# Gated attention: value products one step later, behind the transpositions, and both behind the gate burst

## The chip, the cores and the metric

The kernel runs on one core of a Trainium2 chip. The metric is the time of one execution on the device in microseconds (us). The core has five engines that run side by side and meet only at semaphores: TensorE (PE; its weight loads are shown apart, as PEld), VectorE (DVE), ScalarE (ACT), GpSimd (POOL) and SyncE (SP), which issues most of the transfers here.

## The reference

The program computes two transformer blocks one after the other on 1024 tokens of width 1024. The change lies in the second block, in the mixer that runs three kinds of attention and gates what they give:

```
for h in 4 heads:   fox:    p = softmax(causal(q k^T / 8 + decay));   y = p v
for h in 4 heads:   lstm:   w = (q k^T) * exp(decay);  y = w v / max(|w 1|, floor), then an RMS norm
for h in 8 heads:   window: p = softmax(band(q k^T / 8 + bias), sink); y = p v      # 128 keys back
gates = sigmoid(h @ w_gates)              # [1024 tokens, 4 * 1024]
merged = sum over 4 branches of gate * (y_branch @ w_branch)
```

The products `h @ w_gates` are the large ones of this stage. They need no attention result, so the kernel runs them between the steps of the attention.

## The kernel before

The function `gated_attention` holds the stage. It has one stream of instructions for each engine, written out by hand, and semaphores between them.

**Steps.** There are N = 128 steps, one for a block of 128 queries of one head: steps 0 to 31 are the fox heads, 32 to 63 the decay heads (`lstm`), 64 to 127 the window heads. A step t of a fox head has t + 1 blocks of 128 keys, a window step has two (the first of a head has one). On TensorE a fox or window step has three parts. `score` makes the scores of a step in PSUM. `turn_probs` transposes its probabilities, block by block, into the PSUM tile `turned`. `multiply` makes the value products from the transposed copy `pt` (shown as `ga_row` in the trace). A decay step has `score` and then `add_up`, with no transposition.

**Other engines in a step.** VectorE's `shift` reads the scores and writes the tile `probs` (shown as `ga_p`); the next `score` waits for it (`shifted`), since there is one tile of scores. ScalarE's `exponentials` work in place on `probs`, and ScalarE's `copy_turned` copies `turned` to `pt`. In a decay step VectorE's `weigh` takes the place of `shift`. After each head, VectorE scales the eight results (`scale_head`) or divides them (`divide`); the first product of the next head waits for that.

**Gate bursts.** The gate products are 112 products of 4 chunks; a chunk is three matmuls of 512 columns (high and low parts of both operands, lines 238 to 240). The 448 chunks are cut into 131 bursts, and `gates(s + 1)` is the burst of step s, with 3 or 4 chunks:

```
bounds = [N_GATE * PART * i // BURSTS for i in range(BURSTS + 1)]
ends = [max(i for i in range(BURSTS) if bounds[i] <= q * PART + PART - 1) - 1 for q in range(N_GATE)]
split_at = {step: q + RING for q, step in enumerate(ends) if q + RING < N_GATE}
```

The weights of a product stand in a ring of two (`RING = 2`) as a high and a low part. ScalarE casts the high part of product q + 2 (`high_part`, line 4160) in the step in which product q ends, and VectorE subtracts it for the low part (`low_part`, line 4257). A product's first chunk waits for its low part (`lows`) and for the evacuation of the product two before it.

**Order on ScalarE.** In step s it goes through these, each where the step has it: row copies, `copy_turned(s - 1)`, `exponentials(s)`, `leave` (evacuates every fourth product of the first half), `high_part`, `swap_high` (casts a part of the tokens' blocks). VectorE's order is `shift(s)`, the head's scaling, the norm, gains and convolution where they fall, `leave`, `low_part`, `swap_low`.

**Order on TensorE.** It can be read at the end of the block for `nc.tensor` below: `score(s)`, `turn_probs(s - 1)`, `gates(s + 1)`, `multiply(s - 1)`, and at some steps `turn_rows`, which transposes finished rows.

Of the kernel before, what the change touches and what calls it, by code (L numbers as in the profile page):

```python
# [33 lines left out]
ST = S // P  # L34
# [3673 lines left out]
def gated_attention(k, HT, v2, vm, biases, sinks, fox_y, ml_y, swa_y, first_gates, lower):  # L3708

    nc = k.nc  # L3710
    HEADS, N = 4, SLOTS
# [3 lines left out]
    with k.phase() as ctx:  # L3715
# [36 lines left out]
        rows_a = k.X[:, 0:2, :].rearrange("p a (t n) -> p (a t) n", n=4 * HD)  # L3752
# [14 lines left out]
        def kind_of(n):  # L3767
            return "fox" if n < 4 * ST else "lstm" if n < 8 * ST else "window"
# [22 lines left out]
        def head_target(g):  # L3791
            if g == 0:
                return k.first_fox_head_in, 16 * 8
            loads = sum(8 if h < 4 else 6 if h < 8 or h % 4 == 0 else 2 for h in range(2 - g % 2, g + 1, 2))
            return head_in[g % 2], 16 * loads
# [5 lines left out]
        BURSTS = N + 3  # L3801
# [17 lines left out]
        for n in range(4):  # L3819
            c, tokens = swaps[n]  # L3820
# [44 lines left out]
                return evacuated, m + 1  # L3865
            return added, adds_of(m, q - first_of(m)) if m < PAIRS else adds_of(m, {A22_T4: 1, S3_T3: 3, S4_B22: 4}[i])

        y_groups = [("fox", rows_a, fox_y, c, q, 35 + 2 * c + q, 1 + 2 * c) for c in range(2) for q in range(2)]
        y_groups += [("lstm", rows_b, ml_y, c, q, 71 + 2 * c + q, 4) for c in range(2) for q in range(2)]
        y_groups += [("window", (rows_a, rows_b)[c // 2], swa_y, c, q, 64 + 16 * (c + 1) + 2 + q, 8 + 2 * c + 2)  # L3870
                     for c in range(4) for q in range(2)]
# [183 lines left out]
        @block.tensor  # L4055
        def _(pe):
            def score(n):
                g, t = n // ST, n % ST
                pe.wait_ge(*head_target(g))
                if n:  # L4060
                    pe.wait_ge(shifted, n)
                width, key = (S - t * P, t * P) if kind_of(n) == "lstm" else (chunks_of(n) * P, first(n) * P)
                own, other, other_low, own_again = own_of(g), other_of(g), other_low_of(g), own_again_of(g)
                for at in range(0, width, HALF):
                    to = min(at + HALF, width)
                    nc.tensor.matmul(scores[:, at:to], own[:, t * P:(t + 1) * P], other[:, key + at:key + to],
                                     start=True, stop=False)
                    last = nc.tensor.matmul(scores[:, at:to], own_again[0:HD + 4, t * P:(t + 1) * P],
                                            other_low[0:HD + 4, key + at:key + to], start=False, stop=True)
                last.then_inc(products, 1)  # L4070

            def turn_probs(n):
                pe.wait_ge(exps, n + 1)
                pe.wait_ge(copied, turned_count(n))
                if n == 8 * ST:
                    pe.wait_ge(scaled, 8)
                for c in range(chunks_of(n)):
                    last = nc.tensor.transpose(turned[:, c, :], probs[n % 2][:, c * P:(c + 1) * P], k.ident[:])
                last.then_inc(turns, 1)

            def multiply(n):
                g, t = n // ST, n % ST
                pe.wait_ge(copied, turned_count(n) + 1)
                if t == 0 and g:
                    pe.wait_ge(scaled, g)
                col = g * HD if g < 4 else 4 * HD + (g - 8) // 4 * HD
                for c in range(chunks_of(n)):
                    last = nc.tensor.matmul(head_out[:, t, :], pt[:, c, :], v2[:, first(n) + c, col:col + HD],
                                            start=(c == 0), stop=(c == chunks_of(n) - 1))
                last.then_inc(values, 1)  # L4090

            def add_up(n):
                g, t = n // ST, n % ST
                pe.wait_ge(shifted, n + 1)
                if t == 0:
                    pe.wait_ge(scaled, g)
                    pe.wait_ge(copied, 4 * ST)
                for c in range(t + 1):
                    last = nc.tensor.matmul(lstm_out(t), w[c][:, (t - c) * P:(t - c + 1) * P], vm[:, c, g - 4, :],
                                            start=(c == 0), stop=(c == t))  # L4100
                last.then_inc(values, 1)

            def lstm_out(t):
                return turned[:, t // 4 * 4:t // 4 * 4 + 4, :].rearrange("p c n -> p (c n)")[
                    :, t % 4 * (HD + 1):(t % 4 + 1) * (HD + 1)]

            def turn_rows(i):
                kind, rows, _, c, q, _, ready = y_groups[i]
                pe.wait_ge(normed if kind == "lstm" else scaled, ready)
                if i:  # L4110
                    pe.wait_ge(*y_evacuated(i - 1))
                for t in range(4):
                    last = nc.tensor.transpose(y_turned[:, t, :], rows[:, 4 * q + t, c % 2 * P:(c % 2 + 1) * P], k.ident[:])
                last.then_inc(y_turns, 1)

            def gates(burst):
                for x in range(bounds[burst], bounds[burst + 1]):
                    q, c = x // PART, x % PART
                    m, i = gate_order[q]
                    chunks, tokens = block_of[i]  # L4120
                    if c == 0:
                        pe.wait_ge(lows, q + 1)
                        if q >= 2:
                            pe.wait_ge(*evacuation(q - 2))
                        if m in (0, PAIRS) and i in swap_of:
                            pe.wait_ge(k.block_lows, swap_of[i])
                        if m == PAIRS and i == S4_B22:
                            pe.wait_ge(k.blocks_in[2], 32)
                    last = add_product(nc, gate_ps[q % 2][:], part(weights[q % RING], slice(None), c, slice(None)),
                                       part(part(HT, slice(None), chunks, tokens), slice(None), c, slice(None)), c == 0, c == PART - 1)  # L4130
                    if c == PART - 1:
                        last.then_inc(gate_products, 1)

            gates(0)
            for s in range(END):
                if s < N:
                    score(s)
                if 1 <= s <= N and kind_of(s - 1) != "lstm":
                    turn_probs(s - 1)
                if s + 1 < BURSTS:  # L4140
                    gates(s + 1)
                if 1 <= s <= N:
                    if kind_of(s - 1) == "lstm":
                        add_up(s - 1)
                    else:
                        multiply(s - 1)
                if s in y_at:
                    turn_rows(y_at[s])

# [101 lines left out]
        def _(dve):  # L4251
# [61 lines left out]
            def weigh(n):  # L4313
                g, t = n // ST, n % ST
                dve.wait_ge(products, n + 1)
                dve.wait_ge(exps, n + 1)
                dve.wait_ge(values, g * ST)
                width = S - t * P
                nc.vector.scalar_tensor_tensor(out=w[t], in0=scores[:, 0:width], scalar=HD ** -0.5, in1=probs[n % 2][:, 0:width],
                                               op0=ALU.mult, op1=ALU.mult).then_inc(shifted, 1)  # L4320
# [75 lines left out]
            for s in range(END + 1):  # L4396
                if s < N and kind_of(s) != "lstm":
                    shift(s)
                if s + 1 < N and kind_of(s + 1) == "lstm":
                    mask(s + 1)  # L4400
                if s < N and kind_of(s) == "lstm":
                    weigh(s)
                if s % ST == 1 and s > ST:
                    g = s // ST - 1
                    if 4 <= g < 8:
                        divide(g)
                    else:
                        scale_head(g)
                for h in range(4):
                    if s == (4 + h + 1) * ST + 3:  # L4410
                        mean_square(h)
                    if s == (4 + h + 1) * ST + 5:
                        normalise(h)
                if s - 1 in y_at and y_groups[y_at[s - 1]][0] == "lstm":
                    gain_rows(y_at[s - 1])
                if s in conv_step:
                    convolve(*conv_step[s])
                if s in evac_at:
                    leave(evac_at[s])
                if s in split_at:  # L4420
                    low_part(split_at[s])
                if s in swap_at:
                    for part_index in swap_at[s]:
                        swap_low(part_index)
# [957 lines left out]
```

## Time and profile before

| | us |
|---|---|
| median of the runs (3) | 3155.11 (3154.7 to 3161.17) |
| the profiled execution's own time | 3152.55 |
| its span, first to last instruction | 3150.6 |
| the gated attention stage in it | about 1738 to 2276 |

All of it comes from one profiled execution. Times in the rows are us from the start of the span, durations in us unless marked ns. The share PEclk is the clock that TensorE was granted: 1.00 is 2.4 GHz, and the lower level is 1.2 GHz, so a stretch with both has a value between 0.5 and 1.

### The profile page before, as it was taken

How to read it: one execution, taken by the hardware profiler on the slowest of the kernel's cores; microseconds unless marked ns; L12 is line 12 of the kernel's file. 1: busy time of each engine (PE TensorE's matmuls, PEld its weight loads, DVE VectorE, ACT ScalarE, POOL GpSimd, SP SyncE). 2: the span in 40 equal slices, each digit the busy share in tenths (PEclk: the TensorE clock that was granted, in tenths of full speed). 3: DMA queues.
4: the chain of work that ended last, by engine and by line, in shares of the span. 5: the costliest groups of instructions: out<-in, count | busy, mean ns of one | idle time of the engine just before them, and what ended most of it. 6: DMA issues, size and time to landing. Idle time of an engine off the chain costs nothing. (4 is left out here: it accounts for less than half of the span.)

```text
span 3150.6 us, 40756 instructions
## 1 busy us (share of the span) xinstructions
PE 2950.7 (94%) x14913; PEld 2454.7 (78%) x14913; DVE 1993.9 (63%) x2874; ACT 1568.3 (50%) x2502; POOL 557.5 (18%) x452
## 2 busy tenths in 40 slices
PE   7998999898969999969999999989999899999999
PEld 6766999686858888858777888777787778888887
DVE  5436888523768888874542445565576676666685
ACT  5325788533548888864531444434444332323443
POOL 0001210000233333321422111123200032222000
PEclk9999999899979999989999999999999999999999
DMA  3344221302168888763354545477664233333643
GB/s 110 88 133 121 61 61 32 114 21 103 61 236 297 288 298 289 279 214 111 114 167 130 135 126 163 144 241 224 205 229 141 67 100 109 107 101 114 240 154 114
DMA packets 304553, 475.69 MB, mean 151 GB/s; under 512 B 48675, under 2 KB 196202, under 8 KB 291814
## 3 DMA queue, kind: packets, MB, share of 16 engines
q1 hardware_dynamic: 279718, 427.70, 42.7%
q10 hardware_dynamic: 9088, 28.58, 2.3%
q0 software_dynamic: 15552, 16.82, 1.9%
q8 instruction: 121, 1.98, 0.3%
q14 instruction: 74, 0.61, 0.1%
HBM read 410.55 MB, written 125.87 MB: 170 GB/s over the span
## 5 line engine op out<-in xcount | busy, mean ns | idle before, releaser
L2856 DVE TENSOR_TENSOR moe_wgu_low<-moe_raw,moe_wgu_high 128x2048 fp32r<-128x2048 f32 x94 | 211.2, 2289 | 47.3 <-ACT moe_wgu_high L2793 45.2
L238 PE MATMUL ga_gate<-second_h_high,ga_ws_high 128*128 128x512 f32 x448 | 190.2, 425 | 15.2 <-DVE ga_ws_low L4257 12.2
L2793 ACT ACTIVATE moe_wgu_high<-moe_raw 128x2048 fp32r<-128x2048 f32 x92 | 171.3, 1910 | 20.2 <-ACT moe_y L2802 20.2
L239 PE MATMUL ga_gate<-second_h_low,ga_ws_high 128*128 128x512 f32 x448 | 179.5, 401 | 0.0
L240 PE MATMUL ga_gate<-second_h_high,ga_ws_low 128*128 128x512 f32 x448 | 179.5, 401 | 0.0
L2964 POOL DMA_INDIRECT moe_rows<-scratch_ffn_rows,slot_of_block x47 | 110.5, 2351 | 223.5 <-PE moe_turned L2746 120.0
L238 PE MATMUL up_bank<-second_h_high,up_w_high 128*128 128x512 f32 x352 | 138.7, 394 | 10.5 <-DVE up_w_low L3574 7.3
L238 PE MATMUL pr_acc<-second_h_high,pr_ws_high 128*128 128x512 f32 x336 | 137.8, 410 | 4.9 <-DVE pr_stage L3291 4.1
L240 PE MATMUL up_bank<-second_h_high,up_w_low 128*128 128x512 f32 x352 | 138.4, 393 | 0.0
L239 PE MATMUL up_bank<-second_h_low,up_w_high 128*128 128x512 f32 x352 | 138.2, 393 | 0.0
L240 PE MATMUL pr_acc<-second_h_high,pr_ws_low 128*128 128x512 f32 x336 | 131.9, 393 | 0.0
L239 PE MATMUL pr_acc<-second_h_low,pr_ws_high 128*128 128x512 f32 x336 | 131.8, 392 | 0.0
L3616 DVE TENSOR_TENSOR X<-X,up_bank 128x512 f32<-128x512 f32 x132 | 90.7, 687 | 63.4 <-PE up_bank L240 59.9
L4283 DVE TENSOR_TENSOR ga_stage<-ga_stage,ga_gate 128x512 f32<-128x512 f32 x96 | 65.8, 685 | 95.5 <-PE ga_gate L240 59.1
L238 PE MATMUL down_acc<-second_h_high 128*128 128x512 f32 x300 | 116.7, 389 | 0.0
L239 PE MATMUL down_acc<-second_h_low,second_h_high 128*128 128x512 f32 x300 | 116.7, 389 | 0.0
L240 PE MATMUL down_acc<-second_h_high,second_h_low 128*128 128x512 f32 x300 | 116.7, 389 | 0.0
L2812 ACT ACTIVATE moe_down_ws_high<-moe_raw_down 128x1024 fp32r<-128x1024 f32 x94 | 99.7, 1062 | 31.6 <-PE moe_down L240 31.6
L1687 ACT ACTIVATE twin_pt<-twin_turned 128x512 f32<-128x512 f32 (+1 forms) x192 | 86.8, 487 | 55.8 <-PE twin_turned L1573 54.6
L238 PEld LDWEIGHTS ga_gate<-second_h_high,ga_ws_high 128*128 128x128 f32 x448 | 87.2, 195 | 32.1 <-DVE ga_ws_low L4257 13.5
L2867 DVE TENSOR_TENSOR moe_down_ws_low<-moe_raw_down,moe_down_ws_high 128x1024 fp32r<-128x1024 f32 x94 | 110.6, 1217 | 1.8 <-ACT moe_down_ws_high L2812 1.7
L238 PE MATMUL up_bank<-up_t_high,up_w_high 128*128 128x512 f32 x264 | 103.0, 390 | 1.4 <-DVE up_w_low L3574 1.4
(676 smaller groups left out, 8608.1 us busy)
## 6 DMA issues: line engine op xcount, KB each, us to landing
moe_raw<-in_w_expert_gate_dram SPq DMA_DIRECT2D x32, 1024.0 KB, 5.0
moe_raw<-in_w_expert_up_dram SPq DMA_DIRECT2D x32, 1024.0 KB, 7.1
moe_raw_down<-in_w_expert_down_dram SPq DMA_DIRECT2D x32, 1024.0 KB, 7.4
scratch_gates<-ga_stage SPq DMA_DIRECT2D x96, 256.0 KB, 3.2
scratch_expert_rows<-moe_y ACTq DMA_DIRECT2D x46, 512.0 KB, 5.1
ga_w<-in_w_in_dram SPq DMA_DIRECT2D x92, 256.0 KB, 3.7
scratch_hidden<-X SPq DMA_DIRECT2D x77, 256.0 KB, 2.2
down_rows<-scratch_hidden SPq DMA_DIRECT2D x73, 256.0 KB, 2.9
```

What stands on the lines that cost most here:

```text
L238: nc.tensor.matmul(out, w[0], x[0], start=start, stop=False)
L239: nc.tensor.matmul(out, w[0], x[1], start=False, stop=False)
L240: return nc.tensor.matmul(out, w[1], x[0], start=False, stop=stop)
L1687: nc.scalar.activation(turned_sb[p % 4][:, 0:end - start, :], turned[p % 2][:, 0:end - start, :], ACT.Copy).then_inc(copied, 1)
L2793: nc.scalar.activation(wgu[i % 2][0][:, :, m, :], raw[(2 * i + m) % RAW][:].rearrange("p (c n) -> p c n", n=FF), ACT.Copy).then_inc(up_hig ...
L2812: nc.scalar.activation(w_down[0][:, c * D:(c + 1) * D], raw_down[i % RAW_DOWN][:, c * D:(c + 1) * D], ACT.Copy).then_inc(down_highs, 1)
L2856: nc.vector.tensor_tensor(wgu[i % 2][1][:, :, m, :], raw[(2 * i + m) % RAW][:].rearrange("p (c n) -> p c n", n=FF), wgu[i % 2][0][:, :, m, ...
L2867: nc.vector.tensor_tensor(w_down[1][:, c * D:(c + 1) * D], raw_down[i % RAW_DOWN][:, c * D:(c + 1) * D], w_down[0][:, c * D:(c + 1) * D], ...
L2964: k.nc.gpsimd.indirect_dma_start(out=rows[i % 2][:], out_offset=None, in_=k.scratch["ffn_rows"], in_offset=bass.IndirectOffsetOnAxis(ap=sl ...
L3616: nc.vector.tensor_tensor(out, x, bank_at(f, bank_i), ALU.add).then_inc(combos, 1)
L4283: nc.vector.tensor_tensor(stage[t][:], prior[:], bank[:], ALU.add).then_inc(added, 1)
```

## The change

In the loop over the steps TensorE's order becomes `score(s)`, `gates(s + 1)`, `turn_probs(s - 1)`, `multiply(s - 2)`, and then `add_up(s - 1)` for a decay step. The scaling of fox and window heads moves one step later, and the row transpositions of the fox heads wait for one more scaling in the count. Waits that would close a circle in the first decay head are dropped: `weigh` and `add_up` wait for values and scaling only from the second decay head on.

```
@@ y_groups
-        y_groups = [("fox", rows_a, fox_y, c, q, 35 + 2 * c + q, 1 + 2 * c) for c in range(2) for q in range(2)]
+        y_groups = [("fox", rows_a, fox_y, c, q, 35 + 2 * c + q, 2 + 2 * c) for c in range(2) for q in range(2)]
@@ add_up
                 if t == 0:
-                    pe.wait_ge(scaled, g)
+                    if g > 4:
+                        pe.wait_ge(scaled, g)
                     pe.wait_ge(copied, 4 * ST)
@@ block.tensor, the loop over s
                 if s < N:
                     score(s)
+                if s + 1 < BURSTS:
+                    gates(s + 1)
                 if 1 <= s <= N and kind_of(s - 1) != "lstm":
                     turn_probs(s - 1)
-                if s + 1 < BURSTS:
-                    gates(s + 1)
-                if 1 <= s <= N:
-                    if kind_of(s - 1) == "lstm":
-                        add_up(s - 1)
-                    else:
-                        multiply(s - 1)
+                if 2 <= s <= N + 1 and kind_of(s - 2) != "lstm":
+                    multiply(s - 2)
+                if 1 <= s <= N and kind_of(s - 1) == "lstm":
+                    add_up(s - 1)
                 if s in y_at:
                     turn_rows(y_at[s])
@@ weigh
-                dve.wait_ge(values, g * ST)
+                if g > 4:
+                    dve.wait_ge(values, g * ST)
@@ block.vector, the loop over s
-                if s % ST == 1 and s > ST:
-                    g = s // ST - 1
-                    if 4 <= g < 8:
-                        divide(g)
-                    else:
-                        scale_head(g)
+                if s % ST == 1 and 4 * ST < s - ST < 8 * ST:
+                    divide(s // ST - 1)
+                if s % ST == 2 and s > ST and not 4 * ST < s - ST < 8 * ST:
+                    scale_head(s // ST - 1)
```

## Rows read from the trace of the kernel before

**Rows 1.** Windows: stretch, length, busy time (instructions) by engine, PEclk, DMA share, GB/s.

```profile
1738.00:1886.00 148.00, 145.34 (x871) 127.11 (x870) 65.95 (x125) 72.28 (x141) 18.25 (x15) 1.00 0.49 131
2021.00:2276.00 255.00, 232.09 (x1234) 196.31 (x1233) 149.31 (x306) 105.29 (x274) 69.01 (x51) 0.95 0.71 215
```

**Rows 2.** Waits of TensorE's weight loads, 1735 to 2275: total, times, longest.

```profile
PEld ga_gate L238 <- DVE ga_ws_low L4257: 7.1, 2, 5.8
...
PEld ga_out L4088 <- ACT ga_row L4182: 4.0, 3, 2.5
...
PEld ga_turned L4078 <- ACT ga_p L4188: 1.2, 4, 0.4
```

**Rows 3.** Timeline, a fox step: start, us, engine, line, operation, tiles, count.

```profile
1803.68 0.19 PEld L4066 LDWEIGHTS ga_scores<-x_rounded 128*128 128x128 f32 x1
...
1804.49 0.92 PEld L4078 LDWEIGHTS ga_turned<-ident,ga_p 128*128 128x128 f32 x7
...
1805.69 0.92 ACT L4182 ACTIVATE ga_row<-ga_turned 128x896 f32<-128x896 f32 x1 [2.27 <-PE ga_turned L4078]
...
1806.50 1.14 ACT L4188 ACTIVATE ga_p<-ga_p,ga_least 128x1024 f32<-128x1024 f32 x1
...
1807.54 0.19 ACT L4188 ACTIVATION_READ_ACCUMULATOR ga_p<-ga_p,ga_least 128x1 f32 x1
...
1808.04 1.75 PEld L4088 LDWEIGHTS ga_out<-v,ga_row 128*128 128x128 f32 x14
```

**Rows 4.** Timeline, window steps.

```profile
2149.68 0.69 DVE L4283 TENSOR_TENSOR ga_stage<-ga_stage,ga_gate 128x512 f32<-128x512 f32 x1 [8.33 <-DMA ga_stage<-scratch_gates]
...
2151.41 0.51 ACT L4188 ACTIVATE ga_p<-ga_p,ga_least 128x256 f32<-128x256 f32 x1 [3.27 <-DVE ga_least L4300]
...
2151.82 0.19 ACT L4188 ACTIVATION_READ_ACCUMULATOR ga_p<-ga_p,ga_least 128x1 f32 x1
...
2151.91 0.62 ACT L4160 ACTIVATE ga_ws_high<-ga_w 128x512 fp32r<-128x512 f32 x1
...
2152.56 0.69 DVE L4257 TENSOR_TENSOR ga_ws_low<-ga_w,ga_ws_high 128x512 fp32r<-128x512 f32 x1
...
2156.25 0.65 PEld L4088 LDWEIGHTS ga_out<-v,ga_row 128*128 128x128 f32 x4
...
2156.82 0.19 PEld L4066 LDWEIGHTS ga_scores<-x_rounded 128*128 128x128 f32 x1
...
2157.07 0.25 PEld L4078 LDWEIGHTS ga_turned<-ident,ga_p 128*128 128x128 f32 x2
...
2157.59 0.38 ACT L4182 ACTIVATE ga_row<-ga_turned 128x256 f32<-128x256 f32 x1 [0.22 <-PE ga_turned L4078]
...
2157.86 0.19 PEld L238 LDWEIGHTS ga_gate<-second_h_high,ga_ws_high 128*128 128x128 f32 x1
...
2158.55 0.19 PEld L238 LDWEIGHTS ga_gate<-second_h_high,ga_ws_high 128*128 128x128 f32 x1
```

**Rows 5.** Timeline, where the first decay head follows the fox heads.

```profile
1886.66 1.23 DVE L4319 SCALAR_TENSOR_TENSOR swa_y<-ga_scores,ga_p 128x1024 f32<-128x1024 f32 x1 [2.75 <-PE ga_out L4088]
...
1888.00 0.19 PEld L4066 LDWEIGHTS ga_scores<-x_rounded 128*128 128x128 f32 x1 [1.62 <-issue]
```

**Rows 6.** Windows behind three stalls of TensorE; PEclk is the third last column.

```profile
1888.10:1891.50 3.40, 3.40 (x10) 2.82 (x11) 2.67 (x6) 1.22 (x3) 0.00 (x0) 0.61 0.60 157
...
2028.10:2031.50 3.40, 3.40 (x10) 2.66 (x11) 0.00 (x0) 0.76 (x3) 0.00 (x0) 0.60 1.01 333
...
1749.10:1752.00 2.90, 2.68 (x15) 2.34 (x16) 2.20 (x6) 1.71 (x4) 1.51 (x2) 1.00 0.24 90
```

**Rows 7.** Timeline, the first transposition of the window heads.

```profile
2027.99 0.14 PEld L4078 LDWEIGHTS ga_turned<-ident,ga_p 128*128 128x128 f32 x1 [2.44 <-issue]
```

**Rows 8.** Timeline, the first swap of token blocks.

```profile
1745.74 2.00 ACT L4167 ACTIVATE second_h_high<-fox_y 128x1024 fp32r<-128x1024 f32 x2
...
1746.81 2.36 DVE L4264 TENSOR_TENSOR second_h_low<-fox_y,second_h_high 128x1024 fp32r<-128x1024 f32 x2 [0.26 <-ACT second_h_high L4167]
...
1749.29 0.19 PEld L238 LDWEIGHTS ga_gate<-second_h_high,ga_ws_high 128*128 128x128 f32 x1 [1.43 <-issue]
```

**Rows 9.** Timeline, the scaling of the last window head.

```profile
2271.37 0.69 DVE L4335 TENSOR_TENSOR X<-ga_out,ga_inverse 128x512 f32<-128x512 f32 x1
```

## The prediction

> **What bounds the kernel now.** I read the busy times of the three parts of the gated attention stage first [rows 1]. In its first part (the fox heads, 148 us) TensorE is busy for 145.34 us and its clock is full; in the last part (the window heads, 255 us) for 232.09 us at a mean granted clock of 0.95. The reader is to see that TensorE's stream is nearly full, so an order of its instructions can win back only stalls that exist. The waits of TensorE's weight loads name them [rows 2]: 1.2 us in four waits of the transpositions for ScalarE's exponentials, 4.0 us in three waits of the value products for its copies, and 7.1 us in two waits of gate products for the low part of their weights. The first two kinds are what the new order can shorten. The third it can lengthen, since ScalarE casts those weights behind its copy and its exponentials.
>
> The timelines show why the present order costs so little. In a step with eight blocks the transpositions end at 1805.41 (1804.49 + 0.92), the copy starts at 1805.69, the exponentials at 1806.50, both under the gate burst, and the value products start at 1808.04 with their copy long there [rows 3]. In a window step the copy starts at 2157.59, while gate loads run until 2159.24 [rows 4].
>
> **The change part by part.** Value products are the same 528 matmuls, transpositions the same 264: no work is added or removed. Only order and waits move. SyncE and GpSimd issue the same transfers and sums in the same order; those that wait for a low part or a value product start later with it, and I price that in the range.
>
> *Gains.* (a) The first decay head no longer waits for the last value product of the fox heads. Before, VectorE's weighting started at 1886.66 after those products, and the scores' weight load stood 1.62 us [rows 5]. Right behind it the clock fell: 0.61 granted over 3.4 us, and the same in the 3.4 us from 2028.1 [rows 6]. At 1.2 GHz instead of 2.4 some half of such a stretch is lost, 1.7 us. So 1.62 + 1.7 = 3.3 us. (b) The first transposition of the window heads waited 2.44 us for the last division [rows 7]. It now stands behind a gate burst, which is 2.3 us or more (3 to 4 chunks of 0.69 us, the distance of the gate loads 2157.86 and 2158.55 [rows 4]), so nearly all of it goes, with its slow stretch: 2.4 + 1.7 = 4.1 us. (c) The four waits for exponentials go: 1.2 us. (d) Of the 4.0 us for copies [rows 2] I count 1.5. The longest, 2.5 us, lies where VectorE waited 8.33 us for a transfer until 2149.68 [rows 4]; the next score product needs VectorE's shift behind that anyway, so there the stall moves and does not go. Gains: 3.3 + 4.1 + 1.2 + 1.5 = 10.1 us.
>
> *Loss 1, the ring of two weight pairs.* ScalarE's list for a step is untouched: copy of step s-1, exponentials of s, cast of the weights of product q+2 (where q is the product that ended in this step). The copy now waits for transpositions that stand behind the gate burst; so the exponentials, the cast and VectorE's low part all stand behind it too. From the end of the transpositions' loads to the earliest gate load of product q+2 a window step needs: 0.27 to the copy (2157.32 to 2157.59), 0.28 for it (the instructions of a row of ScalarE follow 0.1 us closer than their durations), 0.41 for the exponentials, 0.09 for reading the sums, 0.65 until VectorE starts, 0.69 for the low part, and about 0.1 to hand over (1887.89 to 1888.00 [rows 5]): 2.5 us [rows 4]. TensorE has meanwhile: value products 0.57 (2156.25 to 2156.82), scores 0.25 (to 2157.07), and 4-k gate chunks of 0.69, where k is how many chunks of the burst follow the end of product q; the other product of the ring takes 4 chunks, k of them in this burst. That is 0.82 + 0.69(4-k): 2.89 us for k=1, 2.20 for k=2, 1.51 for k=3. So k=0 and k=1 are hidden, k=2 stalls 0.3 us and k=3 1.0 us.
>
> The bursts follow from the code: 448 chunks over 131 bursts. In the window steps k=3 comes 7 times and k=2 15 times. With each step's own block count (a first block of a head is narrower, one early cast stands behind an evacuation of 0.5 us) I get 7.3 + 5.6 = 12.9 us. In the fox steps a copy of c blocks takes 0.07 + 0.107c and the exponentials 0.19 + 0.106c (through 0.38 and 0.92, and 0.41 and 1.04), against 0.25 a block of value products (1.75 for seven) and 0.116 a block of scores (0.81 for seven) [rows 3, 4]. Value products grow faster than the copies, so wide steps hide more: four k=3 give 3.1 us, six k=2 2.4, one k=1 with an evacuation in front 0.4, together 5.9. Decay steps have no transposition and stay. Loss 1: 18.8 us.
>
> *Loss 2, the first swap of token blocks.* In step 1 ScalarE casts two parts (2.00 us) behind its weight cast, VectorE makes the low parts until 1749.17 (1746.81 + 2.36), and a gate product waits until 1749.29 [rows 8]. Now the copy of step 0 waits for gate loads that end near 1745.9; copy, exponentials and weight cast move the two casts from 1745.74 to about 1747.5, so the product waits 1.8 us longer.
>
> *Loss 3, the end.* The last value products now follow the last burst, and the last division (0.69 us [rows 9], its two small predecessors, the products' own way out: 1.5 us, an estimate) stands bare in front of the last row transpositions. Before, it ran under that burst.
>
> *The removed waits* of decay head 0 are free. The head scaling moves one step with its products and has the cover it had.
>
> Sum: 18.8 + 1.8 + 1.5 - 10.1 = +12.0 us. Against the profiled execution's own 3152.55 us (its span 3150.6 and 1.95 around it) that is 3164.5; the median of the runs is 3155.11, 2.56 above, so I give 3167.1. Bounds: loss 1 could be 0 if no cast were late, or 18.8 plus a slow stretch of the clock behind each of the 11 places with k=3 (19 us more). A slow stretch came behind 1.62 us of idleness, but none behind the 1.43 us of [rows 8]: the clock granted from 1749.1 on is 1.00 [rows 6]. A stall of 1.0 us is nearer to the second, so I take none.
>
> On the clock the Trainium skill's page "TensorE: Matmul & The Clock Gate" (HAM oscillation — how this bites in real kernels) names only long idle gaps, of a transfer's length, as what brings the lower clock. By that the gains lose their two slow stretches, 3.4 us, and the change would come to 3170.5; the trace disagrees, with 0.61 behind a gap of 1.62 us.
>
> **Rivals.** *Faster:* the cast is not late. For this the chain of 2.5 us must be below 1.51, the whole of k=3. It speaks for it that three of the chain's six parts are hand-overs; against it that every part is read from a row. Then only losses 2 and 3 remain: 3155.1 + 3.3 - 10.1 = 3148.3; with these hidden too, 3145.0. The point of decision is the first gate load behind a k=3 burst, such as in steps 68, 75, 82: no idle before it. *No change:* the stalls of k=3 alone appear (3.1 + 7.3 = 10.4) because the small ones of k=2, 0.3 us each, sink in hand-overs: 10.4 + 3.3 - 10.1, 3158.7. *Much slower:* low parts that are 2 to 3 us later delay the weight transfers and GpSimd's sums, which are late already in the longest gate wait, 5.8 us [rows 2], and the clock falls behind some k=3 places: half of 19, plus two such places longer by 2.5 us each: 3167.1 + 14.5 = 3181.6. *The clock gives nothing back:* 3170.5.
>
> **How the numbers follow.** Forecast 3167.1: 0.42. Faster: 0.21. No change: 0.16. Much slower: 0.16. Clock: 0.05. A measurement of this kernel tells some 0.2% (6.3 us) from no change. The forecast, the clock rival and much slower lie above that (0.63, of which I give 0.03 to "same" for a sum that is 6 us too high); the faster rival reaches below it with most of its weight. Faster 0.2, same 0.2, slower 0.6. The range of 8 in 10 goes from 3146 to 3181; the forecast alone, with loss 1 between 12 and 24 us, from 3160 to 3173.
>
> **What would show it.** Right: idle of about 1 us before gate products, released by VectorE's low part, about twenty times in the window and fox parts; ScalarE's copies starting behind each burst; no wait of the transpositions for exponentials; no stall of 1.6 us at the first decay step. Wrong: TensorE's busy share unchanged with no such waits, or the time going to waits of VectorE for partial sums. What would make the prediction wrong is a chain that is shorter than its rows say, or idleness that now comes before a transfer that TensorE would have waited for anyway.

## The result and the profile after

The changed kernel takes 3209.53 us (median of 4 runs, 3206.04 to 3211.66), the kernel before 3157.34 in the same comparison: ratio 1.0163, 95% interval 1.0146 to 1.0181. It is 52 us slower. The forecast was slower, by 12 us, with a range up to 3181: the direction was right, the size was four times too small and outside the range.

The profiled execution has a span of 3204.1 us, 53.5 more than before. I measure the stage from the gate load that follows the wait of 6.43 us at its start to the first load of the next stage (`mb_out`): 1734.70 to 2280.12 before, 545.4 us, and 1736.07 to 2336.05 after, 600.0 us. So all of the loss is in this stage. By its parts (fox, decay, window steps; columns as in [rows 1]):

```profile
1740.05:1917.10 177.05, 154.35 (x856) 128.75 (x854) 63.24 (x126) 67.47 (x137) 17.96 (x14) 0.96 0.41 108
1917.10:2055.10 138.00, 131.79 (x730) 114.59 (x731) 75.59 (x145) 62.79 (x115) 18.89 (x14) 0.96 0.52 142
2055.10:2332.00 276.90, 237.08 (x1216) 191.90 (x1215) 146.44 (x303) 96.05 (x271) 69.65 (x50) 0.95 0.66 200
```

The fox part took 148 us with TensorE nearly full; it now takes 177 with 23 us idle, at 0.96 of the clock instead of 1.00. The window part grew from 255 to 277. The decay part, whose order did not change, hardly grew.

The waits of TensorE's weight loads in the stage, to be held against [rows 2]:

```profile
PEld ga_gate L238 <- DVE ga_ws_low L4257: 61.0, 39, 6.4
PEld ga_out L4088 <- issue: 12.0, 9, 5.2
...
PEld ga_turned L4078 <- ACT ga_p L4188: 0.3, 1, 0.3
```

The wait for a low part was 7.1 us in two; it is 61.0 in 39. One of the 39 is the 6.43 us at the start of the stage, which the window of [rows 2] leaves out and which the kernel before has too: like for like it is 54.6 us in 38. The waits of transpositions for exponentials and of value products for copies are gone, as forecast (1.2 to 0.3 and 4.0 to none). Value products wait for the head's scaling instead, 12.0 us in nine (2.4 us in three before). The same waits seen on the matmuls name the releaser:

```profile
PE ga_out L4088 <- DVE X L4336: 10.1, 9, 5.0
```

A view that stands in none of the rows above names the missed link. ScalarE's waits in the stage, before:

```profile
ACT ga_row L4182 <- PE ga_turned L4078: 113.2, 76, 4.6
```

and after:

```profile
ACT ga_row L4182 <- PE ga_out L4088: 271.1, 94, 6.9
...
ACT ga_row L4182 <- PE ga_turned L4078: 8.2, 2, 4.9
```

The copy `ga_row` is now released by the value products (`ga_out`), no longer by the transpositions. One place in full, step 6 of the fox part (k=3), answers to [rows 3]:

```profile
1770.69 0.81 PEld L4078 LDWEIGHTS ga_turned<-ident,ga_p 128*128 128x128 f32 x6
...
1771.47 1.20 PEld L4088 LDWEIGHTS ga_out<-v,ga_row 128*128 128x128 f32 x10
...
1772.58 0.19 PEld L4066 LDWEIGHTS ga_scores<-x_rounded 128*128 128x128 f32 x1
...
1772.90 0.81 ACT L4182 ACTIVATE ga_row<-ga_turned 128x768 f32<-128x768 f32 x1 [3.99 <-PE ga_out L4088]
...
1773.61 1.03 ACT L4188 ACTIVATE ga_p<-ga_p,ga_least 128x896 f32<-128x896 f32 x1
...
1774.63 0.62 ACT L4160 ACTIVATE ga_ws_high<-ga_w 128x512 fp32r<-128x512 f32 x1
...
1775.28 0.69 DVE L4257 TENSOR_TENSOR ga_ws_low<-ga_w,ga_ws_high 128x512 fp32r<-128x512 f32 x1 [5.23 <-ACT ga_ws_high L4160]
...
1776.03 0.19 PEld L238 LDWEIGHTS ga_gate<-second_h_high,ga_ws_high 128*128 128x128 f32 x1 [1.97 <-DVE ga_ws_low L4257]
```

The transpositions' loads end at 1771.50. By my chain the copy should start 0.27 later. It starts at 1772.90, 0.23 after the last value product load has ended (1772.67). From there on every link is as priced: 0.71, 1.02, 0.65, 0.69. The gate load waits 1.97 us where I had forecast 0.57.

### The profile page after: what moved, and what is told of

It reads as the page before. It is cut to its first block and busy times, and to the rows that moved or that the text cites. A ratio compares the mean times of both kernels' runs of the same rounds, so it can differ in the third digit from the quotient of the medians.

```text
span 3204.1 us, 40756 instructions
## 1 busy us (share of the span) xinstructions
PE 2969.5 (93%) x14913; PEld 2457.6 (77%) x14913; DVE 1987.8 (62%) x2874; ACT 1558.0 (49%) x2502; POOL 559.4 (17%) x452
## 5 line engine op out<-in xcount | busy, mean ns | idle before, releaser
L238 PE MATMUL ga_gate<-second_h_high,ga_ws_high 128*128 128x512 f32 x448 | 188.8, 421 | 50.3 <-DVE ga_ws_low L4257 44.9
L4182 ACT ACTIVATE ga_row<-ga_turned 128x256 f32<-128x256 f32 (+4 forms) x96 | 44.6, 465 | 279.3 <-PE ga_out L4088 271.1
L238 PE MATMUL up_bank<-second_h_high,up_w_high 128*128 128x512 f32 x352 | 138.3, 393 | 10.5 <-DVE up_w_low L3574 7.3
L4257 DVE TENSOR_TENSOR ga_ws_low<-ga_w,ga_ws_high 128x512 fp32r<-128x512 f32 x76 | 58.7, 772 | 135.5 <-ACT ga_ws_high L4160 135.0
```

What stands on the lines that cost most here:

```text
L238: nc.tensor.matmul(out, w[0], x[0], start=start, stop=False)
L4182: nc.scalar.activation(pt[:, 0:chunks_of(n), :], turned[:, 0:chunks_of(n), :], ACT.Copy).then_inc(copied, 1)
L4257: nc.vector.tensor_tensor(weights[q % RING][1][:], quarter(m, weight_of[i]), weights[q % RING][0][:], ALU.subtract).then_inc(lows, 1)
```

## The experiments

All times are medians in us, all ratios are against the kernel before, timed in the same comparison: 3157.34 for the changed kernel, 3158.05 for e1 to e4, 3156.46 for e5 to e8. "Stage" is the length defined above, from one profiled execution. "Idle" is the sum of the gaps of 0.15 us or more between weight loads in the stage, without the last one, in front of `mb_out`. "Lower clock" is the time in the stage at 1.2 GHz by the trace's clock records.

| kernel | us | ratio, 95% interval | stage | idle | lower clock |
|---|---|---|---|---|---|
| before | 3157.34, 3158.05, 3156.46 | | 545.4 | 41.2 | 36.8 |
| changed | 3209.53 | 1.0163 (1.0146 to 1.0181) | 600.0 | 91.4 | 57.3 |
| e1 second copy | 3179.23 | 1.0060 (1.0036 to 1.0084) | 568.1 | 67.9 | 39.0 |
| e2 cast first | 3157.82 | 1.0006 (0.9978 to 1.0035) | 549.2 | 40.8 | 50.8 |
| e3 decay waits only | 3153.21 | 0.9984 (0.9964 to 1.0003) | 539.8 | 38.6 | 31.2 |
| e4 products before burst | 3178.95 | 1.0061 (1.0035 to 1.0087) | 569.8 | 58.9 | 51.0 |
| e5 e4, scaling back | 3151.14 | 0.9983 (0.9963 to 1.0004) | 541.2 | 38.0 | 32.7 |
| e6 casts and swaps first | 3148.02 | 0.9975 (0.9958 to 0.9993) | 535.5 | 38.0 | 23.5 |
| e7 scaling ahead | 3205.37 | 1.0147 (1.0120 to 1.0174) | 594.5 | 91.3 | 44.9 |
| e8 e6 and e7 together | 3146.59 | 0.9967 (0.9950 to 0.9984) | 532.4 | 35.5 | 20.4 |

The rest of the program varied from execution to execution. In the profiled execution of e3, for example, the stage began 18.7 us later than before, though nothing ahead of it differs: that execution had 152.9 us at the lower clock ahead of the stage, the kernel before 115.5, and half of the difference is the 18.7. So the stage leaves out most of this scatter, but it is one execution of each kernel, and its own time at the lower clock may hold scatter too. The stage's differences to the kernel before agree with those of the medians within 4 us.

**e1: a second place for the copy.** The changed kernel, with:

```
+        pt_even = swa_y[:, 1, :].rearrange("p (c n) -> p c n", n=P)
+
+        def copy_of(n):
+            if n < 4 * ST:
+                return (pt_even, pt)[n % 2]
+            return pt[:, n % 2 * 4:n % 2 * 4 + 4, :]
...
-                act.wait_ge(values, n)
+                if n:
+                    act.wait_ge(values, n if n == 8 * ST else n - 1)
...
```

`copy_turned` writes to `copy_of(n)` and `multiply` reads from it.

> The changed kernel, but with two places for the transposed copy, so that a copy no longer waits for the value products of the step before it. Theory A (a copy that waits for the value products just in front of it puts their whole length into the chain copy, exponentials, cast, low part): the chain is then as short as I had priced it blind, the waits of gate products for low parts fall from some 61 us of weight-load waits to 25 +/- 8, and the time from 3209 to 3170 +/- 8. Theory B (the place of transpositions and copies behind the burst is all that matters, the products' own length does not): the waits stay above 50 us and the time above 3195.

The copy starts 0.04 us after the end of the transposition, and 32 waits of gate products for low parts are left, 41.3 us, with the 6.4 us ahead of the stage. The stage is 31.9 us shorter than that of the changed kernel. That is some 60% of the loss, so theory A holds in kind and B falls. In size it missed: 3179 and not 3170, 41.3 us of waits and not 25. Gaps of gate products behind gate products are 40.9 us in the stage, 11.6 before, and 2.1 of the difference belong to loss 2 below: loss 1 without the missed wait is 27.2 us, still 8.4 more than forecast. A window step with k=2:

```profile
2239.16 0.38 PE L4085 MATMUL ga_turned<-ident,ga_p 128*128 128x128 f32 x2
...
2239.27 0.52 PEld L4095 LDWEIGHTS ga_out<-v,ga_row 128*128 128x128 f32 x4
2239.38 0.56 PE L4095 MATMUL ga_out<-v,ga_row 128*128 128x64 f32 x4
2239.58 0.38 ACT L4190 ACTIVATE ga_row<-ga_turned 128x256 f32<-128x256 f32 x1 [2.69 <-PE ga_turned L4085]
2239.72 0.19 PEld L4073 LDWEIGHTS ga_scores<-x_rounded 128*128 128x128 f32 x1
2239.74 0.31 PE L4073 MATMUL ga_scores<-x_rounded 128*128 128x128 f32 x1
```

From the first load of the value products to that of the scores it is 0.45 us (2239.27 to 2239.72). I had counted 0.57, read between the same loads where they stand behind a gate product [rows 4]. The matmuls themselves are as far apart there as here, 0.37 and 0.36 us:

```profile
2156.48 0.56 PE L4088 MATMUL ga_out<-v,ga_row 128*128 128x64 f32 x4
2156.85 0.36 PE L4066 MATMUL ga_scores<-x_rounded 128*128 128x256 f32 x1
```

Behind a gate matmul the first load stands 0.23 us ahead of its matmul, behind transpositions 0.11. So the 0.57 was no more work, but a load that stood earlier, and each such step hides 0.12 us less than I counted. Over some 30 places that is about 4 of the 8.4 us; the rest is not assigned.

**e2: the weight cast first.** The changed kernel; on ScalarE only:

```
             for s in range(END + 1):
+                if s in evac_at:
+                    leave(evac_at[s])
+                if s in split_at:
+                    high_part(split_at[s])
                 if s - 1 in y_at and y_groups[y_at[s - 1]][0] != "lstm":
                     leave_rows(y_at[s - 1])
                 if 1 <= s <= N and kind_of(s - 1) != "lstm":
                     copy_turned(s - 1)
```

(with the same four lines taken out further down).

> The changed kernel, but ScalarE takes the evacuation and the weight cast of a step ahead of the row copies, the copy and the exponentials. Theory A (all of the loss hangs on the cast queued behind the copy): gate products wait for low parts no more than before the change (some 7 to 18 us), the heads' scaling is on time again, and the gains a to d of the prediction show: 3145 to 3152, just under the kernel before. Theory C (the loss comes from the moved transpositions and products themselves, by later transfers, later scaling or the clock): 3175 or more remains.

```profile
PEld ga_gate L238 <- DVE ga_ws_low L4257: 13.0, 3, 6.4
PEld ga_gate L238 <- issue: 8.5, 3, 3.8
...
PEld ga_out L4088 <- issue: 6.4, 3, 3.3
PEld ga_turned L4078 <- ACT ga_p L4188: 2.6, 3, 2.1
```

The 39 waits are 3 (13.0 us; one of 6.4 lies ahead of the stage in every kernel here), and the ratio goes from 1.0163 to 1.0006: within its interval the whole loss is gone. So the loss hangs on the place of the cast in ScalarE's queue: theory C falls. But the time is that of the kernel before and not under it, above theory A's 3152, so the gains did not show.

**e3: the decay head's waits alone.** The kernel before, with the two `if g > 4:` of the change and nothing else.

> The kernel before with one part of the change alone: the first decay head waits neither for the last value product nor for the scaling of the fox heads. Theory A (my gain a): the stall of 1.62 us of the first decay head's second score product goes, with its stretch at the lower clock, so 3.3 us less. Theory D (the stall only moves to the next wait for VectorE, or the stretch at the lower clock comes elsewhere): within 1 us of the kernel before.

4.8 us less, with an interval that just includes no difference. The stage is 5.7 us shorter: 2.6 us less idle time and 5.7 us less at the lower clock. There is no gap at the first decay step any more (the first gap of 1.62 us in the decay part is the second head's). Theory A is the nearer one.

**e4: transpositions and products ahead of the burst.** The changed kernel, with TensorE's order `score(s)`, `turn_probs(s - 1)`, `multiply(s - 2)`, `gates(s + 1)`.

> The changed kernel, but transpositions and the value products of the step before stand ahead of the gate burst, as the transpositions did before the change; the value products are still one step later. Theory A: copy, exponentials and cast run under the burst again, gate products wait for low parts no more than 10 us over the kernel before, and the time is 3145 to 3158. Theory C (the value products one step later are the costly part, by the scaling that follows them): 3175 or more.

The time is theory C's, 3178.95 us. The waits for low parts went as theory A has it (10.5 us in three), but the first products of each head wait bare, for the scaling, as theory C has it:

```profile
PE ga_out L4088 <- DVE X L4336: 26.8, 10, 6.6
PE ga_gate L238 <- DVE ga_ws_low L4257: 9.2, 3, 6.0
```

The change moved the scaling one step later. In that step VectorE does it behind the shift, and without a burst between scores and products nothing covers it.

**e5: e4 with the scaling in its old step.**

> The kernel with transpositions and value products ahead of the burst (the run before last of this kind took 3179), with the scaling of fox and window heads back in the step where it stood before the change. There the ten waits of value products for the scaling (28.8 us of weight loads) stood bare, since the products come before the burst and VectorE scales in the same step. Theory A (the scaling's step is all that was wrong with that order): those waits go, some 25 to 29 us and a few stretches at the lower clock with them, and the time is 3146 to 3156, at or under the kernel before. Theory C (value products a step later are costly in themselves): above 3165.

As theory A has it: no gap before a value product is left in the stage, 3151.14 us. Value products one step later then cost nothing that these runs can tell.

**e6: casts and swaps first.** e2, with `swap_high` of the token blocks ahead of the copy as well.

> The changed kernel with evacuation, weight cast and also the casts of the swapped token blocks ahead of ScalarE's copy. Against the run with the weight cast alone ahead (3157.8): theory A (loss 2 of the prediction is real): the two waits of gate products in steps 1 and 2 shrink from 3.8 and 2.7 us to about 2.0 and 1.4 as before the change, 2 to 4 us less in the stage. Theory F (these waits come from VectorE's own row of work): no difference in those two waits.

The two waits are 2.04 and 1.14 us (3.84 and 2.70 in e2), so loss 2 is real, 3.4 us. The stage shrank by 13.7 us, more than the 2 to 4 expected. The idle time differs by 2.8 us and the time at the lower clock by 27.3, half of which is 13.7. These are single executions: the intervals of the two ratios overlap, so how much of the clock's part belongs to the edit stays open.

**e7: the scaling ahead of the shift**, in the changed kernel, one edit on VectorE.

> The changed kernel with one edit: VectorE scales a finished head ahead of that step's shift instead of behind it. The products that it waits for stand at the end of the step before. Theory A (the first value product of a head waits bare for a scaling that stands behind a late low part and a shift): the waits of value products for the scaling, 12.0 us of weight loads in nine, go, while the waits of gate products for low parts stay near 61 us; 3209 goes to 3193 to 3200. Theory G (the scaling is late since the low part is, and stays so): no more than 3 us won.

Theory A's size is wrong, G is nearer: 4.2 us less, with intervals that overlap. The gaps before value products are 7.0 us in six (12.0 in nine in the changed kernel). Rows of one of them:

```profile
2169.97 0.69 DVE L4257 TENSOR_TENSOR ga_ws_low<-ga_w,ga_ws_high 128x512 fp32r<-128x512 f32 x1 [2.98 <-ACT ga_ws_high L4160]
...
2170.57 1.25 DVE L4329 TENSOR_TENSOR ga_sums<-ga_sums,ga_sink_exp 128x8 f32<-128x8 f32 x1
...
2172.91 0.30 PEld L4088 LDWEIGHTS ga_out<-v,ga_row 128*128 128x128 f32 x2 [0.55 <-issue]
```

VectorE reaches the scaling (line 4336) only behind the late low part of the step before. But the rows hold a second cause: the addition of eight columns in front of it takes 1.25 us. An addition of GpSimd runs beside it. Without one, later in the same trace, it takes 0.16:

```profile
2169.97 1.82 POOL L4038 TENSOR_TENSOR ga_w_odd<-ga_w_odd,ga_w 128x512 f32<-128x512 f32 x1 [6.13 <-DMA ga_w<-in_w_in_dram]
...
2235.85 0.16 DVE L4329 TENSOR_TENSOR ga_sums<-ga_sums,ga_sink_exp 128x8 f32<-128x8 f32 x1
```

The 1.09 us more are larger than the gap of 0.55. The largest of the six gaps, 3.54 us at 2100.91, stands behind the low part of a swapped token block (2.28 us) and not of a weight. So the place of the scaling is worth 5.0 of the 12.0 us (e7), the place of the cast 5.6 (e2, where 6.4 are left), both with the swaps 8.9 (e8, 3.1 left).

**e8: e6 and e7 together.**

> All three repairs of the changed order together: casts and swaps ahead of ScalarE's copy, scaling ahead of the shift. Theory A: what is left of the change's losses is its end (1.5 us), and its gains a to d show: the stage is 5 to 9 us shorter than before, 3147 to 3153. Theory H (the gains do not exist, since stalls of the window part are set by transfers): 3156 to 3162.

3146.59 us, ratio 0.9967, below 1 with its whole interval, though e6 (0.9975) cannot be told from it. The stage is 13.1 us shorter than before, more than the 5 to 9 expected; theory H falls. Idle time is 5.8 us less, time at the lower clock 16.5 us less, in one execution each. So the changed order of TensorE with the two repairs is a third of a per cent faster than the kernel before. Which of these parts pays is not shown: no run puts casts and swaps first in the kernel before.

## Why the prediction was wrong, step by step

**Loss 1 failed, at its first link.** The kind of the loss, low parts that come late behind the burst, was forecast rightly; its size was not. The prediction said "0.27 to the copy (2157.32 to 2157.59)" and counted the value products as time that TensorE "has meanwhile". In the code above `copy_turned(n)` waits for `values` to reach n, since there is one place `pt` for the copy: it waits for the value products of the step before. Before the change these stood ahead of the step's scores and transpositions, so they were done when the transpositions were, and no row showed the wait. Now they stand directly between transpositions and scores, so they delay the copy and hide nothing. With that one correction the same working (no value products in what TensorE has meanwhile, all other durations kept) gives for k=3 in a window step 2.5 - (0.25 + 0.69) = 1.6 us, for k=2 0.9, for k=1 0.2; over all steps about 50 us instead of 18.8. Measured: gaps of gate products behind gate products, with the 6.43 us ahead of the stage in both, are 67.9 us after and 18.0 before, 49.9 more, of which 2.1 belong to loss 2. That leaves 47.8, in 38 waits where I had named about twenty. The cause is shown by e1, which takes away only this wait, and by e2, which takes the cast out of the chain. A second, smaller error in the same term is the 0.57 us for the value products (e1).

**The scaling "has the cover it had" failed too.** The gaps before value products sum to 12.0 us after and 6.4 before; of the 6.4, 4.0 were for copies and 2.4 for the scaling. So the term put at nothing cost 9.6 us. By e2 and e7 the late cast and the scaling's own place have about equal parts in it; e4 and e5 show what the moved scaling costs without a burst in front.

**The clock.** I took no new stretch at the lower clock. There are 20.4 us more of it in the stage (57.3 against 36.8), worth about 10.2. Some of it stands where the new waits are. The longer ones of the stalls are 1.5 to 2.2 us, where 1.0 was the most forecast, and the fox part, which had none of it before, has four stretches: behind the wait of loss 2 (3.46 us), behind stalls of 2.20 us in the first and in the second head, and behind a wait of 1.83 us for the scaling. How much is scatter of a single execution is open. Behind the stalls in steps 6 and 7 of the first fox head (1.97 and 2.20 us) the row is

```profile
1783.50:1786.90 3.40, 3.40 (x15) 2.93 (x14) 0.41 (x1) 0.00 (x0) 1.04 (x1) 0.58 0.21 77
```

Idle (+50.2) and clock (+10.2) make 60.4 us, 5.8 more than the stage's 54.6. The last gap, in front of `mb_out`, is 0.9 us shorter; the rest of the excess is not resolved.

**Loss 2** was right: the wait before the swapped block's product is 3.46 us, 2.0 more than in [rows 8], where 1.8 was forecast.

```profile
1752.20 0.19 PEld L238 LDWEIGHTS ga_gate<-second_h_high,ga_ws_high 128*128 128x128 f32 x1 [3.46 <-issue]
```

**Loss 3** was right, 1.57 us against 1.5, though 0.9 us of it come back in the next wait, that of `mb_out` (5.6 before, 4.7 after):

```profile
2329.50 0.42 PEld L4114 LDWEIGHTS ga_y<-ident,X 128*128 128x128 f32 x4 [1.57 <-DVE X L4336]
```

**The gains.** (b) is there in full: the gap of [rows 7] is gone. (c) is there, 0.9 of 1.2 us. The gap of (a) is mostly still there in the changed kernel (1.27 of 1.62 us), since VectorE comes late to the first weighting, behind a late low part, though no stretch at the lower clock follows it:

```profile
1915.67 0.69 DVE L4257 TENSOR_TENSOR ga_ws_low<-ga_w,ga_ws_high 128x512 fp32r<-128x512 f32 x1 [1.32 <-ACT ga_ws_high L4160]
...
1917.82 0.19 PEld L4066 LDWEIGHTS ga_scores<-x_rounded 128*128 128x128 f32 x1 [1.27 <-issue]
```

In e3, without that, it is worth 5.7 us of the stage (4.8 of the median) against the 3.3 forecast. (d) was given back as waits for the scaling. Together the gains of about 10 us are nowhere shown by themselves: e8 is 9.9 us under the kernel before, but there the repairs and the clock may have a share.

**The rivals.** "Faster" and "no change" fell, since the cast was late. "Much slower" was the nearest. The lower clock behind some of the late low parts did come; its other half did not, since the transfers were not what grew. VectorE's waits for partial sums (`ga_stage` for `scratch_gates`) went from 35.8 to 18.7 us. "The clock gives nothing back" is not borne out by e3, where the stretch behind the first decay step is gone with its gap.

## What to carry to other kernels

When a group of instructions is moved on one engine, list for every instruction that is released by it all semaphores it waits for, also those that no row shows as a wait today: a single buffer's release can come early today and turn into the head of a chain when the buffer's reader moves behind the work that the next writer waits for anyway. Then walk the other engines' queues in their new order of time. Work with a deadline (here the weight cast for a ring of two) must not stand behind an instruction that the move makes late; changing that order on ScalarE was worth the whole loss (1.0163 to 1.0006).

## What the runs showed of the hardware that was not expected

**What brings the lower clock is not the length of the gap alone.** In the kernel before, the scores near the start of each of the four decay heads wait 1.62 us. Behind two of these waits (1888.0 and 1956.9) a stretch at 1.2 GHz begins within 0.9 us, 0.61 of the clock in [rows 6]; behind the other two (1923.8 and 1991.9) none does. Nor does one behind the waits of 2.02 and 1.43 us around 1744 and 1749 [rows 8]. What decides it stays open; no run here isolates it.

**The time at the lower clock scatters in code that did not change.** Outside the stage the ten kernels here are the same, and their profiled executions had 136 to 180 us at the lower clock there, up to 22 us of time. So a difference of 20 or 27 us of it inside the stage, as between the kernel before and the changed one or between e2 and e6, is not a proof that the edit made it.

**A small VectorE instruction can take eight times as long beside GpSimd.** The addition of 8 columns in front of a window head's scaling runs 80 times in the ten traces. In 63 no addition of GpSimd (`ga_w`, 128x512) runs at the same time, and it takes 0.15 to 0.17 us. In 14 one has begun before it: it takes 0.16 us in one of them and 0.28 to 1.27 in the other 13. The low part of a weight takes at most 0.70 us without such a neighbour and up to 1.83 with one. In this stage that adds to the lateness of scaling and low parts, and it falls on other places when the order changes.
